# Output projections of a two-layer diffusion trunk: how their results are closed, and the order of the loads behind them

## The reference, cut to what matters

```python
def rmsnorm(x, g):
    y = x * rsqrt(mean(x * x, axis=-1) + EPS)
    return y * g

yp = mixed @ w_out                                   # the output projection, 1024 x 1024
xp = xp + mod_p[2] * rmsnorm(yp, norm_mix_post)      # gate, norm, add to the trunk
hp = modulate(rmsnorm(xp, norm_ffn_pre), mod_p[3], mod_p[4])   # input of the MLP
xp = xp + mod_p[5] * rmsnorm(square(relu(hp @ w_ffn_in)) @ w_ffn_out, norm_ffn_post)
```

## Time and profile before

| what | value |
|---|---|
| median of 3 runs | 1475.33 us (1475.29 to 1478.77) |
| profiled execution, its own time | 1474.63 us |
| its span, first to last instruction | 1472.8 us |
| mean granted TensorE clock | 0.989 |
| PE busy | 1411.0 us, 96% of the span |
| DVE, ACT, POOL busy | 701.2, 538.2, 572.2 us |

### The profile page before, as it was taken

One profiled execution on the slowest core, in us unless ns is written; L12 is line 12 of the kernel. 1 busy time (PEld: TensorE's weight loads), 2 busy tenths in 40 slices (PEclk: granted clock), 3 DMA queues, 4 the chain that ended last, 5 costly groups with the idle time before them and its releaser, 6 DMA issues.

```text
span 1472.8 us, 19791 instructions
## 1 busy us (share of the span) xinstructions
PE 1411.0 (96%) x7958; PEld 1208.0 (82%) x7958; DVE 701.2 (48%) x1227; ACT 538.2 (37%) x900; POOL 572.2 (39%) x443
## 2 busy tenths in 40 slices
PE   5999999899999999999899999998999999999998
PEld 3876776699898898898677867787989989989986
DVE  4477854632435435435763578626322222222235
ACT  4376804622131131231451367537312312322222
POOL 1431404434253243343242568542542442442440
PEclk9999999999999999999999999999999999999999
DMA  9524254236333333343334200042343212212201
GB/s 348 155 89 143 87 172 143 75 118 137 101 115 114 115 115 115 101 129 114 129 127 152 85 1 1 2 136 65 115 129 100 86 58 86 87 58 86 87 29 72
DMA packets 95026, 153.76 MB, mean 104 GB/s; under 512 B 10764, under 2 KB 49368, under 8 KB 94936
## 3 DMA queue, kind: packets, MB, share of 16 engines
q1 hardware_dynamic: 82432, 145.76, 30.2%
q10 hardware_dynamic: 12504, 6.75, 1.8%
HBM read 149.58 MB, written 2.92 MB: 104 GB/s over the span
## 4 chain that ended last, share of the span: by engine, by line
PE 78%; DVE 6%; POOL 3%; ACT 3%; issue 2%; DMA 2%; DVEq 0%; ACTq 0%; POOLq 0%
PE PS L1568 23%; PE PS L1570 23%; PE PS L1569 23%; POOL WL L1152 2%; PE PS L1619 2%; PE PS L1866 1%; PE PS L1855 1%; DMA RAW<-in_w_ffn_in 1%; DVE X L1303 1%; PE PS L1834 1%; PE PS L1717 1%; PE PS L1835 1%; ACT WH L865 1%; DVE HL L1338 1%; DVE XCB L1299 1%
## 5 line engine op out<-in xcount | busy, mean ns | idle before, releaser
L1152 POOL TENSOR_TENSOR WL<-RAW,WH 128x512 fp32r<-128x512 f32 x340 | 465.6, 1403 | 713.5 <-ACT WH L865 696.1
L1568 PE MATMUL PS<-HH,WH 128*128 128x384 f32 (+1 forms) x1152 | 357.6, 310 | 7.8 <-DVE HL L1338 3.3
L1569 PE MATMUL PS<-HL,WH 128*128 128x384 f32 (+1 forms) x1152 | 355.7, 309 | 0.0
L1570 PE MATMUL PS<-HH,WL 128*128 128x384 f32 (+1 forms) x1152 | 355.7, 309 | 0.0
L865 ACT CAST WH<-RAW 128x1024 fp32r<-128x1024 f32 x170 | 169.2, 1047 | 446.2 <-PE PS L1570 330.9
L1568 PE MATMUL PS<-WH,AH 128*128 128x512 f32 x640 | 250.3, 391 | 0.4 <-DVE AL L1355 0.4
L1570 PE MATMUL PS<-WH,AL 128*128 128x512 f32 x640 | 249.5, 390 | 0.0
L1569 PE MATMUL PS<-WL,AH 128*128 128x512 f32 x640 | 249.3, 390 | 0.0
L1568 PEld LDWEIGHTS PS<-HH,WH 128*128 128x128 f32 x1152 | 218.6, 190 | 17.5 <-issue 10.7
L1569 PEld LDWEIGHTS PS<-HL,WH 128*128 128x128 f32 x1152 | 218.6, 190 | 0.6
L1570 PEld LDWEIGHTS PS<-HH,WL 128*128 128x128 f32 x1152 | 218.4, 190 | 0.0
(11 more groups left out here) (222 smaller groups left out, 1641.1 us busy)
## 6 DMA issues: line engine op xcount, KB each, us to landing
RAW<-in_w_mod SPq DMA_DIRECT2D x43, 1024.0 KB, 5.1
RAW<-in_w_ffn_in SPq DMA_DIRECT2D x32, 1024.0 KB, 5.5
RAW<-in_w_ffn_out SPq DMA_DIRECT2D x32, 1024.0 KB, 4.7
RAW<-in_w_in_even SPq DMA_DIRECT2D x7, 1024.0 KB, 5.2
RAW<-in_w_qkv SPq DMA_DIRECT2D x6, 1024.0 KB, 5.0
RAW<-in_w_out_even SPq DMA_DIRECT2D x4, 1024.0 KB, 4.9
GG<-gates ACTq DMA_DIRECT2D x16, 256.0 KB, 3.8
RAW<-in_w_out_odd SPq DMA_DIRECT2D x4, 1024.0 KB, 4.9
```

What stands on the lines that cost most here:

```text
L1152: ins = nc.gpsimd.tensor_tensor(cut(ring_view(WL, ld, j)), cut(w_view(ld, b)), cut(ring_view(WH, ld, j)).bitcast(f32), ALU.subtract)
L1568: MM(out, wh, xh, start=first, stop=False)
L1569: MM(out, wh, xl, start=False, stop=False)
L1570: return MM(out, wl, xh, start=False, stop=last)
```

## The change

There are six edits.

1. In both layers ACT squares and sums each 512-column `wout` result straight from its PSUM bank, left and right. The left sum is turned into `YSQ` (scaled, with epsilon) by one more small ACT instruction. `post` for these two phases keeps only the root.
2. DVE multiplies the bank by the gate while it moves it to `ACC` (after ACT's square; same line as the copy), so that ACT's copy L1038 and DVE's L1299 are gone there. In layer 1 tiles 0 and 1 of the left half are copied first and multiplied later.
3. For tiles 0 to 2 (`in_bank`) the modulated first half isn't written to `HF` but back to its bank. The bank is given free only after `HL` has been made from it, by a small `memset` of `MARK`.
4. The gate rows are sent out and read in earlier.
5. `tiles(0, 0)` is cut in two: block 0 runs ahead of `T` of tile 3, block 1 between `T` of tile 3 and `T` of tile 4.
6. The load of `w1` blocks 2 and 3 stands ahead of the two `mod` loads; its first block is split at the `pre` step of tile 4, its second at the `cut` step of tile 3.

```diff
@@ ffn @@
         ld = tiles(0, 0)
+        steps[-1]["only"] = (0,)
+        later = dict(steps[-1], only=(1,), split=[])
         T_(ph, TT - 2)
+        steps.append(later)
         T_(ph, TT - 1)
+        ahead_ld = load("acols", src=("w1", layer), col=2 * P)
         mod(*fill.pop(0))
         tiles(0, 1, ld)
-        tiles(2)
+        tiles(2, None, ahead_ld)
@@ schedule, layer 0 @@
     step("gmlp", uses_a=4)
+    gate_out(0, 2, 0)
+    gate_out(0, 2, 1)
     step("ybh", tile=0)
...
     step("ybh", tile=2)
+    gate_in(0, 2, 0)
+    gate_in(0, 2, 1)
     step("ybl", tile=2)
...
@@ schedule, layer 1 @@
+            if nb == 0 and t == 2:
+                gate_in(1, 2, 0)
+                gate_in(1, 2, 1)
             wout(nb, t, j)
-            if nb == 0 and t in (2, 3):
-                gate_in(1, 2, t - 2)
@@ schedule, places of the splits @@
+        if steps[i]["kind"] == "B" and steps[i]["what"] == "wout" and steps[i]["nb"] and rank < 2:
+            place = next(k for k in range(i, len(steps)) if steps[k]["kind"] == ("pre", "cut")[rank] and steps[k]["t"] == TT - 1 - rank)
@@ banks @@
+        def in_bank(s):
+
+            return s["t"] < 3
+
+        def first_rows_of(s):
+
+            if in_bank(s):
+                return m_bank(s["tm"]).rearrange("p (k n) -> p k n", k=4)
+            return HF[:, 0:4, :]
@@ scalar @@
                 elif k == "post":
                     ph, t = s["ph"], s["t"]
+                    if ph % 2:
+                        nc.scalar.activation(STAT[:, t, 1:2], STAT[:, t, 0:1], ACT.Sqrt, scale=1.0 / D, bias=YSQ[:, t, 1:2])\
+                            .then_inc(ysum, 1)
+                        continue
...
-                    upto(act, m_free, u - 1)
-                    nc.scalar.copy(HH[:, 0:4, cols], HF[:, 0:4, :]).then_inc(h_hi, 1)
+                    if in_bank(s):
+                        act.wait_ge(h_mod, 3 * (ph - 1) + t + 1)
+                    else:
+                        upto(act, m_free, u - 1)
+                    nc.scalar.copy(HH[:, 0:4, cols], first_rows_of(s)).then_inc(h_hi, 1)
...
-                    elif s["what"] == "wout" and s["nb"]:
+                    elif s["what"] == "wout":
+                        t, nb = s["t"], s["nb"]
                         act.wait_ge(b_ready[b % 2], b // 2 + 1)
-                        nc.scalar.copy(ACC[:, s["t"], 512:1024], bank).then_inc(b_free[b % 2], 1)
+                        dst = STAT[:, t, 0:1] if nb else YSQ[:, t, 0:1]
+                        scratch = PART[:, :] if s["ph"] == 3 and nb == 0 else junk(1)[:, 0:512]
+                        nc.scalar.activation(scratch, bank, ACT.Square, accum_out=dst).then_inc(y_squared, 1)
+                        act.wait_ge(y_squared, TT * (s["ph"] - 1) + TT * nb + t + 1)
+                        if nb == 0:
+                            link(nc.scalar.activation(YSQ[:, t, 1:2], YSQ[:, t, 0:1], ACT.Identity, scale=1.0 / D, bias=EPSC[:, :]))
@@ vector @@
-                        ins = V_.tensor_scalar(HF[:, f, :], m_bank(u0)[:, P * f:P * f + P], MODC[:, layer, off + 1, f, v:v + 1],
+                        src = m_bank(u0)[:, P * f:P * f + P]
+                        ins = V_.tensor_scalar(src if in_bank(s) else HF[:, f, :], src, MODC[:, layer, off + 1, f, v:v + 1],
                                                MODC[:, layer, off, f, v:v + 1], ALU.mult, ALU.add)
-                    ins.then_inc(m_free[u0 % 2], 1)
+                    if in_bank(s):
+                        ins.then_inc(h_mod, 1)
+                    else:
+                        ins.then_inc(m_free[u0 % 2], 1)
                 elif k == "cut":
                     cols = slice(s["t"] * P, s["t"] * P + P)
                     dve.wait_ge(h_hi, 2 * s["n"] + 1)
-                    V_.tensor_tensor(HL[:, 0:4, cols], HF[:, 0:4, :], HH[:, 0:4, cols].bitcast(f32), ALU.subtract).then_inc(h_lo[0], 1)
+                    rows = first_rows_of(s)
+                    V_.tensor_tensor(HL[:, 0:4, cols], rows, HH[:, 0:4, cols].bitcast(f32), ALU.subtract).then_inc(h_lo[0], 1)
+                    if in_bank(s):
+                        dve.wait_ge(h_lo[0], s["n"] + 1)
+                        V_.memset(MARK[:, :], 0.0).then_inc(m_free[s["tm"] % 2], 1)
...
-                    if what == "wout" and nb == 0:
-                        dve.wait_ge(b_ready[b % 2], b // 2 + 1)
-                        V_.tensor_copy(ACC[:, t, 512 * nb:512 * nb + 512], bank).then_inc(b_free[b % 2], 1)
+                    if what == "wout":
+                        y = ACC[:, t, 512 * nb:512 * nb + 512]
+                        gain = GG[:, int(t > 0), 512 * nb:512 * nb + 512]
+                        dve.wait_ge(y_squared, TT * (s["ph"] - 1) + TT * nb + t + 1)
+                        if s.get("pt"):
+                            V_.tensor_copy(y, bank).then_inc(b_free[b % 2], 1)
+                        else:
+                            if t in (0, 2):
+                                dve.wait_ge(gg_in[nb], 32 * s["ph"])
+                            V_.tensor_tensor(y, bank, gain, ALU.mult).then_inc(b_free[b % 2], 1)
+                        if s["ph"] == 3 and nb == 0 and t in (2, 3):
+                            y, gain = ACC[:, t - 2, 0:512], GG[:, t - 2, 0:512]
+                            upto(dve, b_free, EARLY_OUT[t - 2])
+                            V_.tensor_tensor(y, y, gain, ALU.mult).then_inc(y_late, 1)
@@ tensor @@
-                    order = [(i, part) for i in (0, 1) for part in s["parts"]]
+                    order = [(i, part) for i in s.get("only", (0, 1)) for part in s["parts"]]
```

More of the change, by code:

```diff
@@ L275, in schedule @@
     step("ybh", tile=2)
+    gate_in(0, 2, 0)
+    gate_in(0, 2, 1)
     step("ybl", tile=2)
     mod(*fill[3])
-    gate_out(0, 2, 0)
-    gate_out(0, 2, 1)
     for nb in (0, 1):
@@ L287, in schedule @@
                 mod(0, 4, t // 2)
-            if nb == 0 and t == 1:
-                gate_in(0, 2, 0)
-                gate_in(0, 2, 1)
             if nb == 0 and t in (0, 4):
@@ L508, in hybrid_step @@
         STAT = sb("STAT", [P, TT, 6])
+        YSQ = sb("YSQ", [P, TT, 2])
         EPSC = sb("EPSC", [P, 1])
+        MARK = sb("MARK", [P, 1])
         LG = sb("LG", [P, 4, 8])
@@ L602, in hybrid_step @@
         consts_made = sem("consts_made")
+        y_squared, y_late = sem("y_squared"), sem("y_late")
+        h_mod = sem("h_mod")
         ysum, xsum, x_new, xn_ready, yg_ready = sem("ysum"), sem("xsum"), sem("x_new"), sem("xn_ready"), sem("yg_ready")
@@ L1292, in _ @@
                         dve.wait_ge(a_lo, 16 * ph)
[L1293 to L1298, removed]
-                    V_.tensor_tensor(YG, ACC[:, t, :], gain, ALU.mult).then_inc(yg_ready, 1)
+                    y = ACC[:, t, :]
+                    if ph % 2 == 0:
+                        if nchain > 1:
+                            dve.wait_ge(x_new, nchain - 1)
+                        if t == 0:
+                            for half in (0, 1):
+                                dve.wait_ge(gg_in[half], 32 * ph)
+                        V_.tensor_tensor(YG, y, GG[:, 2 + (t > 0), :], ALU.mult).then_inc(yg_ready, 1)
+                        y = YG
                     dve.wait_ge(ysum, nchain)
                     link(V_.reciprocal(STAT[:, t, 2:3], STAT[:, t, 1:2]))
-                    dve.wait_ge(yg_ready, nchain)
-                    V_.scalar_tensor_tensor(X[:, t, :], YG, STAT[:, t, 2:3], X[:, t, :], ALU.mult, ALU.add).then_inc(x_new, 1)
+                    if ph % 2 == 0:
+                        dve.wait_ge(yg_ready, TT * (ph // 2 - 1) + t + 1)
+                    elif ph == 3 and t < 2:
+                        dve.wait_ge(y_late, t + 1)
+                    V_.scalar_tensor_tensor(X[:, t, :], y, STAT[:, t, 2:3], X[:, t, :], ALU.mult, ALU.add).then_inc(x_new, 1)
                 elif k == "pre":
```

## The result

| | before | after |
|---|---|---|
| median | 1475.79 us (5 runs, 1475.29 to 1478.77) | 1482.77 us (5 runs, 1481.91 to 1484.01) |
| ratio after / before | | 1.0045, 95% interval 1.003 to 1.0059 |
| profiled execution, span | 1474.63, 1472.8 us | 1483.97, 1482.2 us |
| mean granted clock | 0.989 | 0.983 |

The account below looks back on a forecast made before the run. TensorE, busy 96% of the span, bounds the kernel. Each of two stretches takes 0.5 + 19.4 + 0.9 + 8.6 = 29.4 us plus 2.1 lost clock, 3.2 and 3.9 more: 1474.63 + 7.1 = 1481.7 us, range 1476.5 to 1486.5.

Parts of the forecast that it names:

- The wait inside `mod`: Both layers, between `mod`'s 8th and 9th matmul: PE stands some 6 us until the second half lands at 19.4 us.
- The lost clock: Behind the wait inside `mod`, PE's clock drops: 2.1 us lost per stretch, bounds 0 and 3.4.
- The kept bank: Banks held until `HL` is made: `T` of tile 1 waits 0.5 us (0 to 0.9), `T` of tile 3 about 1.6.
- The stretch: Last `wout` group to `tiles(2)`, per layer: 29.4 us at full clock, 31.5 with the lost clock; 3.2 and 3.9 more.
- The gates: Gate rows wanted by DVE about 6 us sooner, also sent sooner; late arrival holds one bank with 8 us to spare.
- The end of layer 0's MLP: Listed with the start and the attention as a stretch of PE waits that the change leaves alone.
- the closings: DVE's chain per tile falls from some 6.7 to about 5.5 us; tiles ready some 2 us sooner, first wait (1.7 us) removed.
- faster: `mod` finds its second half: Rival, chance 0.07: PE reads the second half without the wait; stretches 3 to 5 us less each, 1465 to 1468 us.
- the rival without a lost clock: Rival, chance 0.21: the wait is there but the clock stays up or steps overlap better; 29.4 us each, 1477.6 us.

Follow-up runs that it names:

- both_splits_first: The changed kernel with both blocks of w1's second pair split at the `pre` of tile 4, none behind the `cut` of tile 3: 1480.86 us.
- order_back: The changed kernel with its load of w1's second block pair put back behind `mod`, all else as changed: 1469.49 us.
- casts_behind: The changed kernel with the load back behind `mod` and the next w1 pair's casts behind the emptying of the banks of `tiles(0, 1)`: 1466.29 us.
- no_bank: The changed kernel with `in_bank` false for every tile, so all modulated halves go to `HF`: 1483.05 us.
- order_back_t_back: The changed kernel with the load back behind `mod` and `T` of tile 3 back behind both blocks of `tiles(0, 0)`: 1474.76 us.
- t_between_alone: The kernel before with `T` of tile 3 between the two blocks of `tiles(0, 0)`, PE's loop reading which block to do: 1476.27 us.

## Why the prediction was right, step by step

The time was forecast 1481.7 and measured 1482.77 us, a change of +7.1 against +7.0. The mechanism was right; that the sizes agree to 0.1 us is luck, since the stretches fell 0.8 us short of the forecast and something outside them made up for it, and the interval of the change is 4.4 to 8.7 us. Step by step:

- **The wait inside `mod`** was right in place, order and size: second `WL` done 13.3 us behind the last `wout` group (14.0 forecast), landing at 18.7 and 18.6 (19.4), PE's wait 6.40 and 6.33 us ("some 6"). One link was another: ACT's second cast was done 10.0 us behind the group (277.10), and `WL` began at 10.8, when POOL had finished `HL` of tile 3 (277.92). `both_splits_first` moved the `WL` and the landing followed; `order_back` took the load away and the wait was gone.
- **The lost clock** was forecast as 2.1 us per stretch. `tiles(0, 1)` takes 8.40 us at full clock (`casts_behind`) and took 10.26 and 9.27; the second half of `mod` took 1.86 (start to start) instead of about 0.93. Together 2.8 and 1.8 us, 2.3 on average.
- **The kept bank**: `T` of tile 1 waited 0.82 (0.5 forecast), `T` of tile 3 1.25 (1.6), `mod` 1.41 (1.3). Writing the modulated half to PSUM takes 410 ns as DVE's row has it, 1.37 us for four, against 404 and 1.36 to SBUF: the taken value of 0.34 each from start to start was right. The Trainium skill's sentence (ScalarE: Activation LUTs, Step-by-step) that VectorE lies closer to SBUF has no price here.
- **The stretch**: 30.80 + 0.82 = 31.6 and 29.73 + 0.83 = 30.6, forecast 31.5 each. That is +3.3 and +3.0 us where 3.2 and 3.9 were forecast, 6.3 together instead of 7.1.
- **The rest of the profiled difference.** The spans differ by 9.4 us, 3.1 more than these 6.3. PE's rows, held against those of the kernel before, show where. Some 1.5 us had arisen by 204 us, with a lower clock: at 20 to 40 and at 60 to 80 us 0.74 and 0.91 after, 0.83 and 1.00 before, and 0.83 and 1.00 in `order_back`, which has the same instructions up to there. So I take it for chance in that one execution, which is 1.2 us above its median; why the clock differs isn't shown. About 0.7 us arises between 204 and 208 us, with the gates (next point). The rest, 0.9 us net, is spread over the rest of the run: 1.1 us more at 720 to 730 us, where the clock is 0.83 after and 1.00 before, 0.7 more at 750 us, 0.7 more in smaller pieces, and 1.7 less between 860 and 900 us.
- **The gates.** "A late arrival would hold one bank with 8 us to spare" had the place right, but the slack was used up: the cost wasn't 0. DVE waits 7.97 us for them in layer 0, since their load takes 9.6 us from issue to landing beside the weights' loads, and PE then waits 0.55 us. The rows behind it are 0.7 us later against the kernel before than those ahead of it, in `order_back` as well. Nothing in the forecast's sum stands for this.

```profile
206.86 0.69 DVE L1465 TENSOR_TENSOR ACC<-PS,GG 128x512 f32<-128x512 f32 x1 [7.97 <-DMA GG<-gates]
```

- **The end of layer 0's MLP.** The prediction had the change leave it alone. The kept bank applies there too, and `T` waits 2.5 us for L1384. Without banks it waits 1.9 us for ACT's L967 and 0.9 for DVE's L1483 at the same place (`no_bank`), as in the kernel before, so the wait itself costs nothing.
- **What the forecast did not see** is that its sum is a difference of two larger terms. The load's order costs 13.3 us (1482.77 - 1469.49), and everything else gains 6.4. (Alone, on the kernel before, the load's order costs 11, so the terms don't simply add up.) I had valued the closings by the wait of 1.7 us that they remove and by the earlier chain, and `T` between the blocks not at all by itself. Neither the closings alone (1474.94) nor `T` between alone (1476.27) gains anything that can be told. Together they do (1473.17, interval 0.9969 to 0.9994), and with the banks more (1469.49). With the banks kept, what `T` between the blocks is worth is clear of the noise (`order_back` 0.9944 to 0.9976, `order_back_t_back` 0.9984 to 1.0008). Without them the intervals overlap, and it rests on the profiles: "all" of both layers together is 56.2 us before, 55.8 with `T` between alone, 53.8 with the closings alone and 51.3 with both. No run has the gates' earlier places apart from the closings. With short closings DVE is free when `T` of tile 3 is done, and this `T` comes early only between the blocks.

Of the rivals, "faster: `mod` finds its second half" is what the kernel does once the load is back. It gave 1465 to 1468, `order_back` took 1469.49.

## What to carry to other kernels

A load put ahead of others in a ring of two places changes which work frees each place: follow it to the last instruction that reads the place, through every engine's own order. When an edit moves a step, list what moves with it on the engines that only serve it; here casts that wait for a landing stood in front of the emptying of a bank, and moving them was worth 3.2 us. Two edits that each gain nothing that can be told can still be worth some 3 us together when one frees an engine and the other lets the work reach it sooner, so undo them singly and in pairs.

## What the hardware showed that I had not expected

`HL` on DVE takes 684 ns with its first operand in PSUM while POOL works on its own half. With both operands in SBUF it takes 1.80 us beside POOL (1774 ns in the earlier trace rows; 270.90 in `t_between_alone` above) and 0.69 when POOL is idle. In `order_back`, DVE at 268.56 with POOL at 268.47, then DVE at 273.10 with POOL idle until 273.66:

```profile
268.56 0.68 DVE L1381 TENSOR_TENSOR HL<-PS,HH 128x512 fp32r<-128x512 f32 x1
...
273.10 0.69 DVE L1381 TENSOR_TENSOR HL<-HF,HH 128x512 fp32r<-128x512 f32 x1 [0.69 <-ACT HH L975]
```

```profile
268.47 1.29 POOL L1175 TENSOR_TENSOR HL<-HF,HH 128x512 fp32r<-128x512 f32 x1 [4.45 <-ACT HH L977]
273.66 1.26 POOL L1175 TENSOR_TENSOR HL<-HF,HH 128x512 fp32r<-128x512 f32 x1 [3.90 <-ACT HH L977]
```

So the 1.1 us saved per tile are no faster operand, but the end of a conflict. The Trainium skill (SBUF — State Buffer, SBUF: two separate sides) has this as an exclusive lock between a GpSimd operation that reads SBUF and a VectorE one with two SBUF inputs; these rows agree.

The clock held at 1.00 through waits of 1.24, 1.09, 1.63 and 2.01 us in `order_back`, and fell behind waits of 5.3 and 6.4 us. In the kernel before it fell behind 1.67, 1.70 and 1.62 us, so the length of single waits does not sort the cases. One place shows this best, since it is the same in all the kernels here. At the end of layer 0's MLP a `mod` waits for its second half, from 2.58 to 2.75 us. In five of the fourteen kernels the eight matmuls behind the wait take 1.06 to 1.08 us, the full clock; in six they take 1.90 to 1.94, the half clock; in three something between. The kernel before and `order_back`:

```profile
717.95 1.07 PE L1619 MATMUL PS<-RAW,CL 128*32 128x512 f32 x8 [2.60 <-DMA RAW<-in_w_mod]
```

```profile
715.72 1.90 PE L1676 MATMUL PS<-RAW,CL 128*32 128x512 f32 x8 [2.69 <-DMA RAW<-in_w_mod]
```

So the stretch at 714 to 720 us, which spoke for the rival without a lost clock, could as well have lost it. Two profiled executions can differ by 1 us or so at such a place without any edit being the reason. What sorts the cases isn't shown.
